# Six of eight groups of gated rows turned by VectorE's blocks, and a scan chain one slot longer

## The reference, cut to what matters

```python
y = ssd_chunked(xs * dt[..., None], dt * a, bm, cm)      # two chunks of 128 tokens
y = y + ssm_d[:, None] * xs
y = y.reshape(Bsz, S, SSM_D_INNER) * jax.nn.silu(z)
yg = y.reshape(Bsz, S, SSM_GROUPS, SSM_D_INNER // SSM_GROUPS)
yg = yg * lax.rsqrt(jnp.mean(yg * yg, axis=-1, keepdims=True) + EPS)
return yg.reshape(Bsz, S, SSM_D_INNER) * ssm_norm_w
...
merged = sigmoid(gate_a) * (o_nsa @ w_proj_nsa) + sigmoid(gate_b) * (o_ssm @ w_proj_ssm)
```

## Time and profile before

| | before |
|---|---|
| median of three runs | 2050.88 us |
| the profiled execution's own time | 2047.77 us |
| its span (first to last instruction) | 2046.0 us |
| TensorE busy | 2029.2 us (99%) |
| VectorE busy | 1351.2 us (66%) |
| ScalarE busy | 1032.0 us (50%) |
| GpSimd busy | 209.8 us (10%) |
| granted TensorE clock, mean | 0.998 |

### The profile page before, as it was taken

The page is one execution under the profiler, slowest core; times in us unless marked ns, Lnnn a source line. Parts: engine busy times, 40 slices in busy tenths (PEclk is TensorE's granted clock), DMA queues, the critical chain, the costliest instruction groups (busy, mean ns, idle before and its releaser), DMA issues.

```text
span 2046.0 us, 26545 instructions
## 1 busy us (share of the span) xinstructions
PE 2029.2 (99%) x9450; PEld 1672.2 (82%) x9450; DVE 1351.2 (66%) x1623; ACT 1032.0 (50%) x1451; POOL 209.8 (10%) x362
## 2 busy tenths in 40 slices
PE   9999999999999999999999999999999999999997
PEld 7888888888888888888888888888888888888886
DVE  6755676776665678885678867666557556655664
ACT  5444545555544467764577644454434434434443
POOL 4000010101010011120011111101001000000000
PEclk9999999999999999999999999999999999999999
DMA  8656565656657666666666677766666766666663
GB/s 275 217 166 195 166 200 159 206 163 200 182 174 229 185 196 197 196 187 214 180 185 196 198 239 237 230 210 208 214 196 200 225 193 192 229 202 184 221 216 134
DMA packets 201765, 408.87 MB, mean 200 GB/s; under 512 B 14944, under 2 KB 15040, under 8 KB 200240
## 3 DMA queue, kind: packets, MB, share of 16 engines
q1 hardware_dynamic: 188656, 364.56, 57.5%
q0 software_dynamic: 12816, 42.34, 7.2%
q10 hardware_dynamic: 176, 0.40, 0.1%
HBM read 379.91 MB, written 2.16 MB: 187 GB/s over the span
## 4 chain that ended last, share of the span: by engine, by line
PE 89%; DVE 4%; issue 2%; ACT 2%; DMA 1%; DVEq 1%; POOLq 0%; POOL 0%; ACTq 0%
PE acc L301 28%; PE acc L302 27%; PE acc L303 27%; DVE lo L268 2%; PE tr L336 1%; DMA raw<-w_proj_ssm 1%; PE x L883 1%; PE x L950 1%; PE tr L900 1%; ACT hi L262 1%; PE x L890 0%; PE x L815 0%; PE tr L902 0%; PE tr L905 0%; PE x L957 0%
## 5 line engine op out<-in xcount | busy, mean ns | idle before, releaser
L268 DVE TENSOR_TENSOR lo<-raw,hi 128x1024 fp32r<-128x1024 f32 x688 | 835.4, 1229 | 505.5 <-ACT hi L262 499.4
L262 ACT ACTIVATE hi<-raw 128x1024 fp32r<-128x1024 f32 x688 | 717.9, 1056 | 615.9 <-PE acc L303 551.1
L301 PE MATMUL acc<-hi,LAh 128*128 128x512 f32 x1840 | 731.6, 398 | 0.8 <-DVE lo L268 0.8
L303 PE MATMUL acc<-hi,LAl 128*128 128x512 f32 x1840 | 717.3, 390 | 0.0
L302 PE MATMUL acc<-lo,LAh 128*128 128x512 f32 x1840 | 716.7, 390 | 0.0
L301 PEld LDWEIGHTS acc<-hi,LAh 128*128 128x128 f32 x1840 | 345.5, 188 | 77.6 <-issue 5.1
L303 PEld LDWEIGHTS acc<-hi,LAl 128*128 128x128 f32 x1840 | 345.3, 188 | 72.9
L302 PEld LDWEIGHTS acc<-lo,LAh 128*128 128x128 f32 x1840 | 345.7, 188 | 71.1 <-issue 1.7
L301 PE MATMUL acc<-hi,LBh 128*128 128x512 f32 x896 | 350.1, 391 | 0.5 <-DVE lo L268 0.4
L303 PE MATMUL acc<-hi,LBl 128*128 128x512 f32 x896 | 348.7, 389 | 0.0
L302 PE MATMUL acc<-lo,LBh 128*128 128x512 f32 x896 | 348.7, 389 | 0.0
(11 more groups left out here) (315 smaller groups left out, 1247.4 us busy)
## 6 DMA issues: line engine op xcount, KB each, us to landing
raw<-w_in SPq DMA_DIRECT2D x304, 512.0 KB, 3.9
raw<-w_up SPq DMA_DIRECT2D x128, 512.0 KB, 4.0
raw<-w_down SPq DMA_DIRECT2D x128, 512.0 KB, 4.7
raw<-w_proj_ssm SPq DMA_DIRECT2D x64, 512.0 KB, 4.5
raw<-w_proj_nsa SPq DMA_DIRECT2D x32, 512.0 KB, 4.6
raw<-w_out SPq DMA_DIRECT2D x32, 512.0 KB, 5.5
W<-acs_rows POOLq DMA_DIRECT2D x8, 1024.0 KB, 6.3
W<-TB POOLq DMA_DIRECT2D x48, 128.0 KB, 4.2
```

What stands on the lines that cost most here:

```text
L262: act.activation(hi[:, sl, :, :], raw[:, sl, :, :], ACT.Copy).then_inc(s_hi, 1)
L268: dve.tensor_tensor(lo[:, sl, :, :], raw[:, sl, :, :], hi[:, sl, :, :].bitcast(F32), ALU.subtract).then_inc(s_lo, 1)
L301: pe.matmul(o, xh, wh, start=(k == 0), stop=False)
L303: x = pe.matmul(o, xl, wh, start=False, stop=(k == KT - 1))
```

## The change

It does five things, for groups 0 to 5 unless said otherwise.

1. TensorE's `scan_turn_y` is left out for groups 0 to 5; groups 6 and 7 keep it (group 6 in slot 13).
2. In its place VectorE turns the gated rows in blocks in slot 14 (`turn_y`, `Y` into `ZT`), GpSimd issues four more transfers (`spread_y`, `ZT` into `Y`), and in the next iteration ScalarE in slot 4 weighs them in place (4 activations of 128x256) and writes `LBh` (one of 128x1024), and VectorE in slot 5 writes `LBl` (`split_y`). For group 3 this falls into slots 4 and 5 of `C_PB1`.
3. For groups 0 to 6 `scan_state`, `channel_y0`, `turn_y0`, `channel_y1` and `turn_y1` stand one slot later (5, 6, 7, 8, 9), with the copies, `scan_w`, `scan_squares` and `scan_norm` that belong to them.
4. The tanh of z moves from slot 15 of the iteration before to slot 5 (slot 3 for group 7), its gate to slot 6 (4 for group 7). The gated product and the squares are split into one piece per chunk of tokens. `scan_y1` stands ahead of the first taps in slot 9.
5. `ST` gets its own buffer, shared with `XDS`; `YT` becomes a view of `XDT`. The loops of ScalarE and VectorE over `C_PB1` are written out.

```diff
 # GpSimd
+            def spread_y(g):
+                stage_scan(g)
+                pool.wait_ge(s_yb, g + 1)
+                for a in range(4):
+                    pool.dma_start(TY[:, S * a:S * (a + 1)], TZ[32 * a:32 * (a + 1), :].rearrange("i (b n) -> i b n", b=4)).then_inc(s_ysp, 16)
...
                 spread_rows(t)
-                stage_scan(t)
+                if 0 < t < 7:
+                    spread_y(t - 1)
 # TensorE
             def scan_cb(g):
-                pe.wait_ge(s_e3d, g + 1)
+                if g == 7:
+                    pe.wait_ge(s_e3d, 8)
+                elif g:
+                    pe.wait_ge(s_yg, g)
...
-                hooks = {0: [lambda: scan_cb(g)], 4: [lambda: scan_state(g)]}
+                hooks = {0: [lambda: scan_cb(g)], 5 - (g == 7): [lambda: scan_state(g)]}
...
-                    hooks.update({5: [lambda: channel_y0(g)], 6: [lambda: turn_y0(g)], 7: [lambda: channel_y1(g)],
-                                  8: [lambda: turn_y1(g)], 12: [lambda: scan_turn_y(g)]})
+                    hooks.update({6: [lambda: channel_y0(g)], 7: [lambda: turn_y0(g)], 8: [lambda: channel_y1(g)],
+                                  9: [lambda: turn_y1(g)], 13: [lambda: scan_turn_y(g)] if g == 6 else []})
 # ScalarE
+            def split_y(g, k0):
+                act.wait_ge(s_pg, g + 1)
+                act.wait_ge(s_ysp, 64 * g + 64)
+                for ct in range(4):
+                    v = TYV[:, 2 * ct:2 * ct + 2, :, :]
+                    act.activation(v, v, ACT.Copy, scale=NWs[:, ct:ct + 1])
+                act.drain()
+                act.activation(tokens(LBh, k0), TYV, ACT.Copy).then_inc(s_e3a, 2)
...
+                    hooks[4] = [lambda: split_y(g - 1, 4 * ((g - 1) % 4))] if g not in (0, 4) else []
+                    hooks[5] = hooks[5] + [lambda: z_tanh(g)]
...
-            with act.Fori(0, 2) as i:
-                slots(act, split_hi, C_PB1 + 2 * i, 16, {})
+            for i in range(2):
+                slots(act, split_hi, C_PB1 + 2 * i, 16, {} if i else {4: [lambda: split_y(3, 12)]})
 # VectorE
+            def split_y(g, k0):
+                dve.wait_ge(s_e3a, 2 * g + 2)
+                dve.tensor_tensor(tokens(LBl, k0), TYV, tokens(LBh, k0).bitcast(F32), ALU.subtract).then_inc(s_e3d, 1)
+            def turn_y(g):
+                dve.wait_ge(s_yn, g + 1)
+                for t in range(2):
+                    x = dve.transpose(TZ.rearrange("p (b c t j) -> p t c b j", b=4, c=4, t=2)[:, t, :, :, :],
+                                      Y[:, t, :].rearrange("p (c i b) -> p c b i", c=4, b=4))
+                x.then_inc(s_yb, 1)
...
-                hk[9] = [lambda: taps(m, 1)] + hk.get(9, [])
+                hk[9] = hk.get(9, []) + [lambda: taps(m, 1)]
...
-                slots(dve, split_lo, C, 16, {7: [...
+                slots(dve, split_lo, C, 16, {5: [] if i else [lambda: split_y(3, 12)],
+                                             7: [...
```

More of the change, by code:

```diff
@@ L533, in build @@
         out_rows = out[0].rearrange("(t p) d -> p t d", p=P)
+        Z_CHUNK = [C_X0 + 1] + [C_L1 + 2 * i + 1 for i in range(4)] + [C_L2 + 2 * i + 1 for i in range(3)]
         PAIR = [(c, j) for c in range(2) for j in range(6)] + [(c, j) for c in range(2) for j in (6, 7)]
@@ L1247, in scan_state, with first_squares @@
                 act.activation(ST[:, :], X7[:, :], ACT.Copy).then_inc(s_stc, 1)
+            def first_squares(g):
+                act.wait_ge(s_yh, g + 1)
+                act.activation(ZT[:, 0, :], Y[:, 0, :], ACT.Square, accum_out=SS[:, 0:1]).then_inc(s_ss, 1)
             def scan_squares(g):
                 act.wait_ge(s_yg, g + 1)
[L1251 to L1252 removed]
+                act.activation(ZT[:, 1, :], Y[:, 1, :], ACT.Square, accum_out=SS[:, 1:2]).then_inc(s_ss, 1)
             def scan_norm(g):
@@ L1274, in copy_channels @@
                 act.wait_ge(s_yc, n)
-                act.activation(YT[:, :], X7[:, :], ACT.Copy).then_inc(s_yt, 1)
+                act.activation(YT, X7[:, :], ACT.Copy).then_inc(s_yt, 1)
             def scan_iteration(C, par, e, m, g=None, k0=None):
                 hk = scan_hooks(g, k0) if g is not None else {}
-                hk[7] = [lambda: take(C, par, XR[:, 0, :])] + hk.get(7, [])
-                hk[8] = [lambda: conv(e, m)]
+                hk[7] = [lambda: act.wait_ge(s_zg, g + 1) if g is not None else None, lambda: take(C, par, XR[:, 0, :])] + hk.get(7, [])
+                hk[8] = hk.get(8, []) + [lambda: conv(e, m)]
                 hk[12] = hk.get(12, []) + [lambda: conv_tanh(m)]
-                hk[15] = [lambda: take_z(C + 1, (par + 1) % 2, m)]
+                hk[15] = [lambda: take_z(C + 1, (par + 1) % 2)]
                 slots(act, split_hi, C, 16, hk)
@@ L1651, in scan_split, with z_gate @@
                 dve_split_t(dve, g, LBh, LBl, k0, NWs, banks=(X6, X7), sa=s_e3a, done=s_e3d)
+            def split_y(g, k0):
[7 more added lines that the diff above has]
+                x.then_inc(s_yb, 1)
+            def z_gate(g):
+                dve.wait_ge(s_zt, g + 1)
+                dve.scalar_tensor_tensor(ZT[:, :, :], ZT[:, :, :], 1.0, ZR[:, :, :], ALU.add, ALU.mult)
+                dve.drain().then_inc(s_zg, 1)
             def scan_first(g):
@@ L1658, in scan_first @@
                 dve.tensor_copy(CBB[:, 2, :], X7[:, 2 * P:3 * P]).then_inc(s_cbc, 1)
-                dve.wait_ge(s_zt, g + 1)
-                dve.scalar_tensor_tensor(ZT[:, :, :], ZT[:, :, :], 1.0, ZR[:, :, :], ALU.add, ALU.mult)
-                dve.drain()
             def scan_y0(g):
@@ L1676, in scan_y1 @@
                 dve.drain()
-                dve.scalar_tensor_tensor(Y[:, :, :], Y[:, :, :], 0.5, ZT[:, :, :], ALU.mult, ALU.mult).then_inc(s_yg, 1)
+                dve.scalar_tensor_tensor(Y[:, 1, :], Y[:, 1, :], 0.5, ZT[:, 1, :], ALU.mult, ALU.mult).then_inc(s_yg, 1)
             def scan_hooks(g, k0):
-                a, b, c = (5, 6, 10) if g == 7 else (6, 8, 13)
-                return {0: [lambda: scan_first(g)], 1: [lambda: scan_inputs(g)],
-                        2: [lambda: scan_w(g, 0)], 3: [lambda: scan_w(g, 1)], a: [lambda: scan_y0(g)], b: [lambda: scan_y1(g)],
-                        c: [lambda: scan_split(g, k0)]}
+                hooks = {0: [lambda: scan_first(g)], 1: [lambda: scan_inputs(g)]}
+                if g == 7:
+                    hooks.update({2: [lambda: scan_w(g, 0)], 3: [lambda: scan_w(g, 1)], 4: [lambda: z_gate(g)],
+                                  5: [lambda: scan_y0(g)], 6: [lambda: scan_y1(g)], 10: [lambda: scan_split(g, k0)]})
+                else:
+                    hooks.update({3: [lambda: scan_w(g, 0)], 4: [lambda: scan_w(g, 1)], 5: [lambda: split_y(g - 1, 4 * ((g - 1) % 4))] if g not in (0, 4) else [],
+                                  6: [lambda: z_gate(g)], 7: [lambda: scan_y0(g)], 9: [lambda: scan_y1(g)],
+                                  14: [lambda: scan_split(g, k0)] if g == 6 else [lambda: turn_y(g)]})
+                return hooks
             def scan_inputs(g):
+                dve.drain()
                 dve.wait_ge(s_xt, g + 1)
@@ L1725, in _ @@
                 scan_iteration(C_L1 + 2 * i, C_L1 % 2, 5 + i, XA_X0 + 2 + 2 * i, i, 4 * i)
-            with dve.Fori(0, 2) as i:
+            for i in range(2):
                 C = C_PB1 + 2 * i
-                slots(dve, split_lo, C, 16, {7: [lambda: add_gated(8 * C + 8, C_PB1 % 2, ds(2 * NC * i, NC), None, PT)],
+                slots(dve, split_lo, C, 16, {5: [] if i else [lambda: split_y(3, 12)],
+                                             7: [lambda: add_gated(8 * C + 8, C_PB1 % 2, ds(2 * NC * i, NC), None, PT)],
                                              15: [lambda: add_gated(8 * C + 16, (C_PB1 + 1) % 2, ds(2 * NC * i + NC, NC), None, PT)]})
```

39 lines of the change are left out of this document (26 added, 13 removed).

## The result

| | before | after |
|---|---|---|
| median of the runs, us | 2051.15 (2050.82 to 2053.9, 5 runs) | 2061.07 (2060.31 to 2063.83, 5 runs) |
| span of the profiled execution, us | 2046.0 | 2058.9 |

The account below looks back on a forecast made before the run. TensorE, busy 2029.2 of 2046.0 us, was taken as the bound. The terms -5.5 + 1.0 + 0.4 + 2.2 + 0.1 = -1.8 us, applied to the median 2050.88, gave 2049.1, range 2045.3 to 2054.0.

Parts of the forecast that it names:

- saved by TensorE in six groups: Slots 12 and 13 without the transposes of Y: 0.93 us less in each of six groups, 5.5 us in all.
- waits in iterations 1, 2, 3, 5, 6: TensorE waits 0.2 us before the channel products in each iteration with split_y, 1.0 us in all; upper bound 8.5.
- group 0: Late rows cost 0.7 us before slot 6, an old wait of 0.3 for the state copy goes: net 0.4.
- `C_PB1`: TensorE waits for group 3's LBl before group 6 of the first chunk: 2.2 us taken, at least 1.95.
- last group: Group 6's LBl ends within 0.1 us of when scan_cb of group 7 asks for it: 0.1 us.
- signs of being wrong: C_PB1 shows no wait, iterations 1, 2, 3, 5, 6 longer than 51.1 us, or the clock leaves 1.00.
- GpSimd's 0.3 and 1.7 us: Spread of the x rows: 0.3 us until GpSimd starts, the last of four issues 1.7 us later.
- part 1: VectorE from slot 9: transposes end 0.9 us into the next iteration; with 2.7 to landing, x rows there at 5.6.
- part 2: ScalarE from token rows to state copy: channel products can start at 20.8, want 20.6; 0.2 us wait, bounds 0 and 1.7.
- Rival (b): VectorE's run from slot 9 falls behind, x rows land late, five iterations wait: 2056.6 us, slower; chance 0.14.
- Part 3: Group 0: slot 3's split, at 18.0 into the iteration, is wanted at 17.4; 0.7 us lost, net 0.4.
- VectorE as the wrong place: Skill's rule against the change: if VectorE bound the stage, six groups lose 12.5 us, gain 5.5; given Rival (b)'s chance.

Follow-up runs that it names:

- e16: Kernel after with group 3 turned by TensorE, scan_split in slot 13, last group's z tanh behind state copy, load 5 held until all four x-row transfers landed: 2044.76 us.
- e2: Kernel after without y's four transfers per group, ScalarE waiting for VectorE's turn instead: 2062.98 us, ratio 1.006.
- e13: Kernel after with load 5 of each next chunk held until the first of the four x-row spread transfers has landed: 2052.14 us, ratio 1.001.
- e15: Kernel after with load 5 of each next chunk held until all four x-row spread transfers have landed: 2051.92 us, ratio 1.0004.
- e4: Kernel after with all groups turned by TensorE, so no block turns, transfers or split_y of y: 2052.42 us, ratio 1.0012.
- e6: Kernel after with y's block transposes right behind those of the x rows, ahead of the split of slot 14: 2055.32 us, ratio 1.0022.
- e10: Kernel after with group 3 by TensorE, scan_split in slot 13, last group's z tanh behind state copy, both y transposes ahead of slot 14's split: 2047.51 us.
- e5: Kernel before with scan_split moved from slot 13 to slot 14, behind the split that releases the weight load: 2048.85 us, ratio 0.9994.

## Why the prediction was wrong, point by point

Terms of the sum, each with what the iterations of the profile after give (before and after subtracted):

| term | forecast | measured |
|---|---|---|
| saved by TensorE in six groups | -5.5 | -6.1 (6 x 1.01, read in iteration 4) |
| waits in iterations 1, 2, 3, 5, 6 | +1.0 | +13.1 (2.4, 2.9, 2.4, 2.6, 2.8) |
| group 0 | +0.4 | 0.0 |
| `C_PB1` | +2.2 | +5.3 |
| last group | +0.1 | +1.4 |
| sum | -1.8 | +13.7 |

The rest of the program gave 0.8 back, so the spans differ by 12.9. (Six times 0.93 is 5.6 and not 5.5; this changes nothing.) Two of the prediction's own signs of being wrong came: iterations 1, 2, 3, 5 and 6 are longer than 51.1, and the clock left 1.00.

*What held.* The saving, the end of the transposes (0.97 for 0.9), and GpSimd's 0.3 and 1.7 us.

*The step that failed* is the end of part 1, "2.7 to landing", and its reason in part 2, "I take 0.2, since the landing of 2.7 is from this very stage". The last transfer took 5.3. So the term of the waits, +1.0, was 13.1, and each wait lies above its upper bound of 1.7, which was worked out from a landing of 4.2. The chain of part 2 was right in itself: rows that come 2.7 us late (8.30 for 5.6) on top of a wait of 0.2 make 2.9, and iteration 2 lost 2.86. Only the place was forecast in part: 1.0 and 1.2 us of it are waits for `lo` in slots 4 and 5, and 0.6 is the wait for `ST`. With the rows in time, in e16, they are copied at 5.85 and TensorE's wait for `ST` is 0.35, the iteration 0.46 above iteration 4. Rival (b) had the mechanism and nearly the condition ("if the rows land after 4.2 and not 2.7 us"), but gave it 0.14 and argued against it with the order of y's transfers (e2 shows that these are harmless). What the prediction did not ask was which weight load falls among the four: the order of instructions showed it, since `scan_split` left its place between the transposes and the split of slot 14, and group 0 of the kernel before showed what it does. Part 3 saw that group 0's rows landed late and did not ask why.

*`C_PB1`.* The wait itself was 3.78 us, inside its bounds of 1.95 to 3.95 but far from the 2.2 taken: ScalarE's splits there waited 1.79, 2.89, 2.80 and 0.57 us for `w_proj_ssm`. What no term had is that TensorE's clock fell to half behind that wait. TensorE, then the windows 935:939, 939:939.5, 939.5:940, 941:943 and 943:945 (busy us of PE, PEld, DVE, ACT, POOL, granted clock, DMA share, GB/s), against the earlier trace rows:

```profile
939.27 0.50 PE L305 MATMUL acc<-hi,LBh 128*128 128x512 f32 x1 [3.78 <-DVE LBl L1695]
...
941.22 0.63 PE L307 MATMUL acc<-hi,LBl 128*128 128x512 f32 x1
941.65 0.63 PE L305 MATMUL acc<-hi,LBh 128*128 128x512 f32 x1
...
935.00:939.00 4.00, 0.49 (x3) 0.07 (x1) 2.15 (x2) 2.77 (x3) 0.00 (x0) 1.00 0.62 208
939.00:939.50 0.50, 0.23 (x1) 0.23 (x2) 0.50 (x2) 0.00 (x0) 0.00 (x0) 1.00 0.09 25
939.50:940.00 0.50, 0.50 (x3) 0.35 (x3) 0.50 (x1) 0.00 (x0) 0.00 (x0) 0.71 0.62 201
941.00:943.00 2.00, 2.00 (x6) 1.52 (x6) 0.00 (x0) 0.00 (x0) 0.00 (x0) 0.50 0.61 205
943.00:945.00 2.00, 2.00 (x10) 1.65 (x9) 0.00 (x0) 1.02 (x1) 0.00 (x0) 0.97 0.31 116
```

The granted clock is 1.00 through the whole wait and in the first half microsecond of work; then it is 0.50 until about 943. The matmuls start 0.43 us apart instead of 0.227, and slot 6 takes 4.45 instead of 2.72: 1.73 us more. (The wait and these 1.73 us are more than the 5.3 of the table because the kernel before lost 0.4 us in the same slots.) The Trainium skill, "TensorE: Matmul & The Clock Gate", section "What's actually happening", has 1.2 GHz as the clock of an idle TensorE. The trace agrees on the level, 0.50 of 2.4 GHz, and that it follows idleness, but not on the moment: here the idle TensorE kept 1.00 for all of its 3.78 us, and the fall came when it was working again.

*Group 0.* The 0.7 us for `lo` came (slot 5 took 3.82, 0.64 more than in iteration 4), but slot 6 gave 0.31 back (3.95 for 4.26) and the 0.34 that group 0 lost there before is gone: nothing net.

*The last group.* It has late rows and a state copy late in turn, 1.1 us of waiting; with the rows early it takes 50.6 as before, in e13 and e15 with the tanh of z where the change put it, in e16 with it behind the copy.

*VectorE as the wrong place.* The Trainium skill, "VectorE: DVE Perf Modes", section "Rules for kernel authors", would keep the turn on TensorE. The loss did not come from VectorE's 2.08 us as such: e4, without them, has the late rows too, and e16, with them in five groups, is faster than before. They cost only where they stand ahead of the split of slot 14, 0.9 us per iteration in e6 and e10.

*Still open.* That the load among the transfers delays them is shown by e5, e6, e13 and e15; how it does so is not. The Trainium skill, "DMA: Bandwidth & Descriptors", section "Queues, rings and completion order", says that each DMA engine takes turns between the queues by packets; it fits that only transfers still on their way when the load comes are slowed, but no run here shows single packets. Nor is it clear why the last transfer took 3.6 us before and 4.9 in e13, with the load 0.83 and 0.84 us behind the start of its issue. Also open is why in e16 iteration 3 still waits 0.3 us in slot 5 and 0.6 in slot 6, though its rows are copied at 5.86.

## What to carry to other kernels

A landing time read as the median of many transfers is not the landing of the one that is waited for: take each by itself, and look at what other queues issue beside it. When an instruction leaves its place in an order, ask which transfers its neighbours release and where these now fall. A large load can be held back by a semaphore for nothing if its consumer is far enough away: here one wait on SyncE took the kernel after from 2061.1 to 2051.9 (e15), level with the kernel before. Moving work on VectorE, with group 3 back on TensorE, reached 2047.5 (e10), and both kinds of step together 2044.8 (e16). The wait is not for nothing everywhere: behind group 3 and on load 2 it cost more than it gave.
